# Weight sums behind two lower parts, a head's scaling one slot later, a split ahead of a square

## The reference

```python
for l in range(DEPTH_2):
    h = h + 0.5 * swiglu(rmsnorm(h, ffn1_norm[l]), ffn1_w_gate[l], ffn1_w_up[l], ffn1_w_down[l])
    proj = rmsnorm(h, mix_norm[l]) @ w_in[l]
    ...
    y_ret = retention_group(rq, rk, rv, rg, ret_gn_w[l])
    y_diff = diff_attention_group(dq, dk, dv, diff_subln_w[l], ...)
    h = h + jnp.concatenate([y_ret, y_diff], axis=-1) @ w_out[l]
    h = h + 0.5 * swiglu(rmsnorm(h, ffn2_norm[l]), ffn2_w_gate[l], ffn2_w_up[l], ffn2_w_down[l])
h = rmsnorm(h, final_norm)
return h[:, N_META:]

def swiglu(x, w_gate, w_up, w_down):
    return (jax.nn.silu(x @ w_gate) * (x @ w_up)) @ w_down

# the end of the differential attention, one of four heads:
o = o * lax.rsqrt(jnp.mean(o * o, axis=-1, keepdims=True) + EPS) * subln_w
o = o * (1.0 - lambda_init)
```

## Time and profile before

| | |
|---|---|
| Median of three runs | 3046.74 us |
| The profiled execution's own time | 3046.71 us |
| Its span, first to last instruction | 3045.0 us |
| PE busy | 3025.1 us (99%) |
| PE weight loads busy | 2762.7 us (91%) |
| VectorE busy | 2122.1 us (70%) |
| ScalarE busy | 1451.9 us (48%) |
| GpSimd busy | 191.5 us (6%) |
| Mean granted TensorE clock | 0.998 |
| HBM traffic | 114 GB/s over the span |

### The profile page before, as it was taken

How to read it: one execution, slowest core, us unless ns; L and a number is a source line. 1 busy time by engine, 2 the same in 40 slices (tenths; PEclk the granted TensorE clock), 3 DMA queues, 4 the chain that set the end, 5 groups by cost and what they waited for, 6 DMA issues and landing times.

```text
span 3045.0 us, 55707 instructions
## 1 busy us (share of the span) xinstructions
PE 3025.1 (99%) x20552; PEld 2762.7 (91%) x20552; DVE 2122.1 (70%) x3137; ACT 1451.9 (48%) x2554; POOL 191.5 (6%) x237
## 2 busy tenths in 40 slices
PE   9999999999999999999999999999999999999998
PEld 7778887888888799999999999999999999989998
DVE  5545645773576488877667788868887776788876
ACT  4454424442343265634752455535554465355542
POOL 1000000000000011100000011001110000001100
PEclk9999999999999999999999999999999999999999
DMA  4111222222222266533111476335653321247633
GB/s 161 63 63 63 104 97 98 91 96 97 97 90 97 83 162 181 144 119 104 63 63 63 128 188 177 113 111 167 176 158 111 105 70 63 70 144 191 172 111 119
DMA packets 131033, 347.94 MB, mean 114 GB/s; under 512 B 14798, under 2 KB 16334, under 8 KB 130752
## 3 DMA queue, kind: packets, MB, share of 16 engines
q1 hardware_dynamic: 103536, 292.34, 27.9%
q0 software_dynamic: 27056, 53.16, 10.0%
q10 hardware_dynamic: 288, 0.31, 0.0%
HBM read 343.58 MB, written 2.17 MB: 114 GB/s over the span
## 4 chain that ended last, share of the span: by engine, by line
PE 80%; issue 16%; DVE 2%; ACT 1%; POOL 1%; DVEq 0%; POOLq 0%; DMA 0%; ACTq 0%; SPq 0%
PE ps L2586 26%; PE ps L2706 10%; PE ps L2978 9%; PE ps L2975 8%; PE ps L2976 8%; PE ps L3044 6%; PE ps L3333 3%; PE ps L2723 1%; PE ps L3026 1%; PE ps L3027 1%; PE ps L3028 1%; PE ps L2791 1%; PE ps L3111 1%; PE ps L2650 1%; PE ps L2779 0%
## 5 line engine op out<-in xcount | busy, mean ns | idle before, releaser
L825 ACT ACTIVATE w_hi<-w_raw 128x1024 fp32r<-128x1024 f32 (+1 forms) x326 | 341.7, 1048 | 582.1 <-PE ps L2586 266.8
L1541 DVE TENSOR_TENSOR w_lo<-w_raw,w_hi 128x1024 fp32r<-128x1024 f32 (+1 forms) x334 | 404.0, 1210 | 208.2 <-ACT w_hi L825 201.9
L2586 PE MATMUL ps<-h_hi,w_hi 128*128 128x512 f32 (+1 forms) x832 | 274.6, 358 | 0.3
L2586 PE MATMUL ps<-h_lo,w_hi 128*128 128x512 f32 (+1 forms) x832 | 273.8, 357 | 0.0
L2586 PE MATMUL ps<-h_hi,w_lo 128*128 128x512 f32 (+1 forms) x832 | 272.6, 356 | 0.0
L3111 PE MATMUL ps<-h_hi,w_hi 128*128 128x264 f32 (+1 forms) x864 | 253.8, 294 | 1.2 <-DVE mix L2298 1.1
L3111 PE MATMUL ps<-h_hi,w_lo 128*128 128x264 f32 (+1 forms) x864 | 245.1, 284 | 0.0
L3111 PE MATMUL ps<-h_lo,w_hi 128*128 128x264 f32 (+1 forms) x864 | 244.7, 283 | 0.0
L1182 ACT ACTIVATE h_spare<-ps 128x264 f32<-128x264 f32 (+1 forms) x304 | 118.3, 389 | 136.6 <-PE ps L2978 136.5
L3111 PEld LDWEIGHTS ps<-h_hi,w_hi 128*128 128x128 f32 x864 | 162.6, 188 | 12.0 <-issue 7.9
L2978 PE MATMUL ps<-t_hi,w_lo 128*128 128x264 f32 (+1 forms) x608 | 173.2, 285 | 0.0
(11 more groups left out here) (477 smaller groups left out, 8708.0 us busy)
## 6 DMA issues: line engine op xcount, KB each, us to landing
w_raw<-in_stream SPq DMA_DIRECT2D x384, 512.0 KB, 3.3
s_raw<-in_stream SPq DMA_DIRECT2D x152, 256.0 KB, 4.3
s_raw<-in_stream POOLq DMA_DIRECT2D x152, 256.0 KB, 3.8
tmp<-in_stream SPq DMA_DIRECT2D x76, 256.0 KB, 4.8
w_raw<-in_stream SPq DMA_DIRECT2D x32, 256.0 KB, 2.6
w_mix<-in_stream SPq DMA_DIRECT2D x24, 256.0 KB, 3.4
w_mix<-in_stream SPq DMA_DIRECT2D x12, 512.0 KB, 4.6
w_mix<-in_stream POOLq DMA_DIRECT2D x24, 256.0 KB, 4.7
```

Source lines behind the costliest of these rows:

```text
L825: nc.scalar.activation(w_hi[:, s, 0:n], w_raw[:, s, 0:n], ACT.Copy).then_inc(hi_done, 1)
L1541: V.tensor_tensor(w_lo[:, s, 0:n], w_raw[:, s, 0:n], w_hi[:, s, 0:n].bitcast(F32), ALU.subtract).then_inc(lo_done, 1)
L2586: last = T.matmul(out[:, p, :], w[:, s, j * P:(j + 1) * P], x[:, k, c0:c1], start=start and j == 0 and r == 0, stop=stop and j == len(ks) ...
```

## The change

Three edits in the order of VectorE's queue. First, ahead of the first seven-product pair of each large feed-forward, the weight sums are made behind the lower parts of s1 and w1 instead of ahead of them. Second, in both mixers the scaling of head h stands in slots 9, 13, 17 and 21 behind the slot's split of weights, instead of at the end of slots 8, 12, 16 and 20. Third, in the last feed-forward alone, the split `d_next(23)` stands between the residual's addition and the square of the last pair, instead of behind the square, its sum and `last_chain(3)`. Nothing is computed differently.

```diff
                 plain_gate(2)
-                sums(0, 0)
                 s1_lower(E0, 0)
                 w1_lower(E0, 0)
+                sums(0, 0)
                 plain_up(2)
...
-                def take(m, y, inc=True):
+                def take(m, y, inc=True, then=None):
                     x = tile(xT, m, n_tok)
                     step = V.scalar_tensor_tensor(x, y, 0.5, x, ALU.mult, ALU.add)
                     if inc:
                         step.then_inc(slot_free[m % 2], 1)
+                    if then is not None:
+                        then()
                     new_x(q, m, x, n_tok, last or m < 2 * D_PAIRS)
...
-                def d_out(p, s, between=None):
+                def d_out(p, s, between=None, then=None):
...
-                    take(2 * p + s, y, inc=p == D_PAIRS)
+                    take(2 * p + s, y, inc=p == D_PAIRS, then=then)
...
-                d_out(2, 1, before_third)
+                early = (which, L) == (1, LAYERS - 1)
+                d_out(2, 1, before_third, then=(lambda: d_next(23)) if early else None)
                 last_chain(3)
-                d_next(23)
+                if not early:
+                    d_next(23)
                 d_next(24)
...
                     if 0 < p < N_MIX - 1:
                         split_lo(*following(half, s))
+                    if n_t in (4, 8, 12, 16):
+                        d_scale(n_t // 4 - 1)
                     if p == SLOT_MT and L < LAYERS - 1:
                         m_scale()
...
                     if p and order[p - 1] >= RG:
                         gate(p - 1)
-                    if 0 <= n_t < ND and n_t % 4 == 3:
-                        d_scale(n_t // 4)
```

## The result

The changed kernel takes 3052.84 us (median of 11 runs, 3050.52 to 3055.59) where the kernel before takes 3046.43 us in the same session (11 runs, 3044.36 to 3046.88): ratio 1.0023, 95% interval 1.0015 to 1.0031. It is slower by 6.4 us; 3053.8 was forecast.

What follows compares the result with a forecast made beforehand. PE's own work was taken to bound the kernel, so only holes in its row count. The terms +7.45 - 1.37 - 0.86 gave +5.2 us, with the clock +7.1, so 3053.8 us; range 3051.2 to 3056.8.

Steps and rivals of the forecast that it cites:

- PE bounds, holes are the price: Whole run: PE is busy 3025.1 of 3045.0 us, so an edit matters only where it opens or closes PE holes.
- Edit 1: First large feed-forward: with the sums behind two lower parts, PE's wait for wx_lo goes, gaining 1.37 us.
- Edit 3: Last feed-forward: the split ahead of the last pair's square ends PE's wait near 3013.01, gaining 0.86 us.
- Slot 16: First layer's mixer: moving the scaling away lets maxima and eviction run earlier, closing a PE hole and gaining 1.09 us.
- Heads 0 and 1: Both mixers: the later scaling delays PE's head transposes by 0.10, 0.13, 0.09 and 0.14 us, 0.46 in sum.
- Head 2: Both mixers: the scaling behind the split delays PE's transposes by 0.70 us in each layer, 1.40 us in sum.
- Head 3: Slot 21 of both mixers: PE waits 3.34 us for the scaling behind rounding and split, 6.68 us in sum.
- The clock: Behind the two 3.3 us holes: PE falls to half clock, costing 0.95 us a layer, 1.9 us in sum.
- full falls: Behind the long holes: half clock costing a full 1.7 us in both layers, giving 3055.3 us.
- no-fall rival: Behind the long holes the clock does not fall: +5.2 us, 3052.0 us; chance 0.20.
- Head 3 in time: Rival for slot 21: the scaling comes before PE wants it, so not slower, 3045.3 or 3043.4 us; chance 0.07.
- one long one: Long fall behind a hole: 6.9 us at half clock, costing 3.4 us; as rival twice, 3058.7 us, chance 0.05.

Runs made afterwards that it cites:

- experiment 1: Changed kernel with the scaling of all heads back at the end of slots 8, 12, 16 and 20: 3042.31 us (before 3046.48), ratio 0.9990.
- experiment 5: Changed kernel with every head's scaling in the same later slot, but ahead of the second eviction and the split: 3042.72 us (before 3046.48), ratio 0.9987.
- experiment 10: Changed kernel with three unused 512-column filler matmuls on PE ahead of head 3's transpose in both mixers: 3050.91 us (before 3046.45), ratio 1.0015.
- experiment 9: Changed kernel with seven unused 512-column filler matmuls on PE ahead of its wait for head 3 in each mixer: 3054.65 us (before 3046.43), ratio 1.0029.
- experiment 4: Changed kernel with head 3's scaling late in the first layer only, back at the end of slot 20 in the second: 3049.11 us (before 3046.45), ratio 1.0008.
- experiment 6: Changed kernel with each scaling one slot later, behind the second eviction but ahead of the split: 3045.64 us (before 3046.43), ratio 0.9997.
- experiment 3: Changed kernel with only head 3's scaling back at the end of slot 20: 3044.52 us (before 3046.48), ratio 0.9993.

## Why the prediction was right

- **PE bounds, holes are the price.** Held in every run: each edit moved the time by the hole it opened or closed, and by the clock behind it.
- **Edit 1**, forecast -1.37: -1.37 by alignment, -1.3 to -1.4 alone. The cover of 0.3 us for ScalarE's later roundings was enough.
- **Edit 3**, forecast -0.86: -0.96 by alignment, -0.9 to -1.0 alone.
- **Slot 16**, forecast -1.09: -1.12 by the distance from head 1's to head 2's transposes, and 1.1 to 1.2 between experiments 1 and 5.
- **Heads 0 and 1**, forecast +0.46 with no wait to see. By alignment the four transposes lose 0.05, 0.13, 0.06 and 0.13, 0.37 in all, but PE makes some of it good again before the next hole: 0.24 is left.
- **Head 2**, forecast 2 x 0.70: 0.65 and 0.64, of which the trace calls 0.44 and 0.42 idle. I had counted from the load at 2556.99; the matmul behind it started 0.11 later, at 2557.10, and that one is what comes late. What the load no longer hides (0.66 instead of 0.60 for the four transposes) gives half of it back.
- **Head 3**, forecast 2 x 3.34: 3.22 for the start, again 0.11 less for the same reason, and 0.05 for the load, 3.27 each.
- **The clock**, forecast 1.9: 1.6 to 1.9 by experiment 10, 1.4 by experiment 9. The sum is met; its split is not. The forecast had 0.95 for each layer; by levels experiment 4 gives 1.3 to 1.6 to the first hole and 0.3 to the second, while the profiled execution shows 1.25 and 1.45. The forecast was a middle value between no fall and full falls, so that the commonest runs lie on it is in part luck. What a fall costs is shown by the table above; when it begins, and so why it differs between executions, stays open. The no-fall rival is refuted by the stretches at half clock that go when the holes are filled. The two holes of 1.1 us of experiment 6 show none. One row was misread: single-column matmuls stand only behind the earlier hole of 2.4 us, not around it; ahead of it are dense ones of 512 columns. The Trainium skill ("TensorE: Matmul & The Clock Gate", Part 1) says that an idle stretch brings half rate until TensorE has been busy again; the holes of 3.07 us agree, those of 1.1 us show none.
- **Head 3 in time**, the rival on the other side: wrong for this order of VectorE's queue, where the rounding's 2.24 us wait for PE came back unchanged. It is right for the other order, experiment 5.

The sum of measured terms without the clock is -1.4 - 1.0 - 1.1 + 0.2 + 1.3 + 6.6 = +4.6, beside 4.6 for experiment 10 by alignment and 4.5 by levels. With 1.4 to 1.9 for the clock it is 6.0 to 6.5, beside 6.1 to 6.3 by levels: nothing larger than the levels' own scatter is left unassigned. The upper end of the forecast's range was added up wrongly: one full fall and one long one make 5.2 + 1.7 + 3.4, so 3057.0 instead of 3056.8; nothing hangs on it.

## What to carry to other kernels

"One slot later" says little on an in-order queue; ask what stands ahead of the moved instruction there, and what that waits for. Here a split ahead waits for a rounding that waits for the very unit of PE whose successor needs the moved result, so PE waits for a chain of 3.3 us that starts only when its own unit has ended. Standing ahead of the eviction and the split in the same slot turned a loss of 6.1 to 6.3 us into a gain of 3.4. And count lateness at the matmul row, not at the load that runs ahead of it.

## What the hardware showed unexpectedly

- A filler matmul of 512 f32 columns took 0.86 us at full clock (6.0 us for seven).
- The 2.1 us between the levels go with the clock at places that no edit touches. Of the windows from 500 and from 1046 us, the profiled execution of before (3046.71 us, upper level) has clock 0.86 and 0.79; that of experiment 4 (3047.03 us, its lower level) has 1.00 in both:

```profile
500.00:512.00 12.00, 10.38 (x35) 6.03 (x34) 7.29 (x9) 4.85 (x9) 0.00 (x0) 0.86 0.21 86
1046.00:1062.00 16.00, 13.26 (x51) 9.11 (x50) 9.52 (x13) 5.96 (x9) 0.00 (x0) 0.79 0.18 63
```

```profile
500.00:512.00 12.00, 10.08 (x40) 5.75 (x39) 7.46 (x9) 4.85 (x9) 0.00 (x0) 1.00 0.27 87
1046.00:1062.00 16.00, 12.31 (x65) 8.72 (x64) 12.15 (x16) 8.14 (x13) 0.00 (x0) 1.00 0.18 61
```

  The same holes of 1.49 and 2.44 us stand there in both. It is the second place that counts: the profile of experiment 10 (3049.38 us, lower level) has 0.86 in the first window and 1.00 in the second, and by alignment the profiles with 1.00 in the second (experiments 3, 4 and 10) are 2.3 us faster across it than that of before. No experiment was made on it.
- A late transfer in one of twelve profiles cost 1.6 us, more than edit 1 gains: a row of a single profile can be an accident.
